# Gate rows of the second projection: split fp32r products against plain fp32 products in 32-column groups of TensorE

## The reference, cut to what matters

```python
# odd_mixer, layer 2 (w_in: 1024 x 5136, the last 16 columns are the gates)
q, k, v, o, z, g = split(h @ w_in)
g = (g + gate_bias).reshape(b, t, 4, MLSTM_HEADS)
gates = (g[:, :, 0], log_sigmoid(g[:, :, 1]), g[:, :, 2], log_sigmoid(g[:, :, 3]))
# mlstm_scan, per chunk of 128 rows
cum = cumsum(lf)
d_log = where(mask, cum_t - cum_s + li_s, -inf)
inter = cum + m
m_t = maximum(inter, max(d_log))
```

## Time and profile before

| | |
|---|---|
| median of three runs | 4188.26 us |
| lowest and highest | 4185.9 and 4190.44 us |
| profiled execution, its own time | 4191.84 us |
| span in the profile | 4190.2 us |
| PE matmul busy | 3694.5 us, 88% of the span |
| DVE, POOL, ACT busy | 2302.2, 1455.7, 1339.0 us |
| granted PE clock, mean | 0.929 |

### The profile page before, as it was taken

The page is one execution under the profiler, slowest core; times in us unless marked ns, Lnnn a source line. Parts: engine busy times, 40 slices in busy tenths (PEclk is TensorE's granted clock), DMA queues, the critical chain, the costliest instruction groups (busy, mean ns, idle before and its releaser), DMA issues. The chain is left out here.

```text
span 4190.2 us, 51199 instructions
## 1 busy us (share of the span) xinstructions
PE 3694.5 (88%) x17280; PEld 2784.6 (66%) x17280; DVE 2302.2 (55%) x3742; ACT 1339.0 (32%) x1955; POOL 1455.7 (35%) x964
## 2 busy tenths in 40 slices
PE   7999966589999999999189699999999968988687
PEld 4788754456666666665178588888877756876575
DVE  4533239756667676765637653333344335777555
ACT  3322225324444444444110132222223223655200
POOL 1100027336777767677203311000100002333243
PEclk8999986679999999999599899999999987999898
DMA  5212128511111111110244332221111115555443
GB/s 183 93 70 69 56 97 288 158 35 31 38 32 37 37 32 38 31 38 23 91 143 179 131 108 72 70 69 68 68 46 51 34 42 167 185 192 203 162 175 115
DMA packets 278209, 393.60 MB, mean 94 GB/s; under 512 B 79612, under 2 KB 167212, under 8 KB 277888
## 3 DMA queue, kind: packets, MB, share of 16 engines
q1 hardware_dynamic: 220256, 303.64, 22.1%
q10 hardware_dynamic: 47392, 50.50, 3.9%
q0 software_dynamic: 10368, 36.97, 2.2%
HBM read 269.71 MB, written 121.20 MB: 93 GB/s over the span
## 5 line engine op out<-in xcount | busy, mean ns | idle before, releaser
L235 PE MATMUL pj_acc<-pj_whi,pj_h_hi 128*128 128x512 f32 x2064 | 813.4, 394 | 22.8 <-DVE pj_h_lo L481 22.8
L237 PE MATMUL pj_acc<-pj_whi,pj_h_lo 128*128 128x512 f32 x2064 | 808.6, 392 | 0.0
L236 PE MATMUL pj_acc<-pj_wlo,pj_h_hi 128*128 128x512 f32 x2064 | 808.4, 392 | 0.0
L1017 DVE TENSOR_REDUCE al_mx<-al_sx 128x1 f32<-128x512 f32 (+1 forms) x960 | 562.3, 632 | 267.3 <-PE al_sx L1094 254.1
L962 ACT ACTIVATE al_e<-al_st 128x1024 f32<-128x1024 f32 x432 | 443.1, 1026 | 577.3 <-PE al_st L1107 567.8
L481 DVE TENSOR_TENSOR pj_h_lo<-pj_hall,pj_h_hi 128x1024 fp32r<-128x1024 f32 x258 | 369.2, 1432 | 352.2 <-ACT pj_h_hi L369 352.2
L431 POOL TENSOR_TENSOR pj_wlo<-pj_wst,pj_whi 128x2048 fp32r<-128x2048 f32 x28 | 128.5, 4588 | 975.8 <-ACT pj_whi L351 975.8
L992 POOL TENSOR_TENSOR al_acc_p<-al_acc_p,al_e 128x1024 f32<-128x1024 f32 x192 | 457.5, 2383 | 19.7
L235 PEld LDWEIGHTS pj_acc<-pj_whi,pj_h_hi 128*128 128x128 f32 x2064 | 391.2, 190 | 106.5 <-DVE pj_h_lo L481 26.2
L237 PEld LDWEIGHTS pj_acc<-pj_whi,pj_h_lo 128*128 128x128 f32 x2064 | 390.6, 189 | 82.4
L236 PEld LDWEIGHTS pj_acc<-pj_wlo,pj_h_hi 128*128 128x128 f32 x2064 | 391.1, 189 | 80.8
(11 more groups left out here) (256 smaller groups left out, 5554.8 us busy)
## 6 DMA issues: line engine op xcount, KB each, us to landing
s_proj<-pj_stage SPq DMA_DIRECT2D x194, 256.0 KB, 2.1
pj_wst<-in_w ACTq DMA_DIRECT2D x28, 1024.0 KB, 5.4
ml_k<-s_proj SPq DMA_DIRECT2D x36, 512.0 KB, 5.7
ml_v<-s_proj SPq DMA_DIRECT2D x36, 512.0 KB, 9.6
mo_in<-s_proj SPq DMA_DIRECT2D x34, 512.0 KB, 5.9
hm_w<-in_ada_w SPq DMA_DIRECT2D x16, 1024.0 KB, 6.6
ml_q<-s_proj SPq DMA_DIRECT2D x32, 512.0 KB, 7.7
s_h<-ml_h POOLq DMA_DIRECT2D x32, 512.0 KB, 5.7
```

The costliest lines, as they stand in the source:

```text
L235: nc.tensor.matmul(out, s_hi, m_hi, start=start, stop=False)
L236: nc.tensor.matmul(out, s_hi, m_lo, start=False, stop=False)
L237: return nc.tensor.matmul(out, s_lo, m_hi, start=False, stop=stop)
L1017: V.tensor_reduce(mx[:, x:x + 1], slots[x % NSX][:, 0:spans[x % NS][1]], AX.X, ALU.max).then_inc(sx_max, 1)
```

## The change

The gate weights become one tile `wg` of 32 columns for each of the eight slices of the inner dimension, not split. The gate product of a tile becomes eight plain fp32 matmuls on `hall` itself: slices 0 to 3 go to the PSUM partitions 0 to 31, 32 to 63, 64 to 95 and 96 to 127, and slices 4 to 7 are added to the same four. So `gacc` holds four partial sums of the 16 gate rows, in 128 rows; the bias goes to the first. `graw` keeps its size. The gate stage loads all four parts (16 transfers in place of four) and adds them, the forget gates on DVE and the input gates on POOL. PE's gate product now waits for `hall` of its tile; ACT's `h_hi` no longer waits for gate products.

```diff
         sg = m.sb(tag + "sg", [P, CH])
-        wg_hi, wg_lo = m.sb(tag + "wg_hi", [P, KD, P], F32R), m.sb(tag + "wg_lo", [P, KD, P], F32R)
+        wg = m.sb(tag + "wg", [P, KD, 32])
         gst, gbias = m.sb(tag + "gst", [P, 2, P]), m.sb(tag + "gbias", [P, 1])
         gacc = m.ps(tag + "gacc")
-        g_ld, g_hi, g_lo = m.sem(tag + "g_ld"), m.sem(tag + "g_hi"), m.sem(tag + "g_lo")
+        g_ld = m.sem(tag + "g_ld")
         g_mm, g_out, g_stored = m.sem(tag + "g_mm"), m.sem(tag + "g_out"), m.sem(tag + "g_stored", 2)
         sg_done, sgz_done = m.sem(tag + "sg_done"), m.sem(tag + "sgz_done")
-        wg_st = hall[:, KP:KP + 2, NT - 4:, :]
-        by_tile = lambda w: w[:].rearrange("p (a b) n -> p a b n", a=2)
     x_ld, stats_done, var_done, rstd_done, xn_done = m.sem(tag + "x_ld", NX), m.sem(tag + "stats_d"), m.sem(tag + "var"), m.sem(tag + "rstd_d"), m.sem(tag + "xn")
...
             eng.wait_ge(w1_hi, 1)
-            if not L0:
-                eng.wait_ge(g_lo, 1)
 
...
                     act.wait_ge(mm_done, k - RING + 1)
-                    if not L0 and k - RING < NT:
-                        act.wait_ge(g_mm, k - RING + 1)
                 nc.scalar.activation(h_hi[:, k % RING], hall[:, :, t, :], ACT.Copy).then_inc(hi_done, 1)
...
             if not L0:
-                for i in range(2):
-                    act.dma_start(wg_st[:, i], a["w_gate"][i * KP * P:(i + 1) * KP * P].rearrange("(k p) n -> p k n", p=P)).then_inc(g_ld, 16)
+                act.dma_start(wg[:], a["w_gate"].rearrange("(k p) n -> p k n", p=P)).then_inc(g_ld, 16)
                 act.dma_start(gbias[:], a["gate_bias"]).then_inc(g_ld, 16)
...
             split_w(1)
-            if not L0:
-                act.wait_ge(g_ld, 48)
-                nc.scalar.activation(by_tile(wg_hi), wg_st, ACT.Copy).then_inc(g_hi, 1)
             modulate(1)
...
                         act.wait_ge(g_mm, t + 1)
+                        act.wait_ge(g_ld, 32)
                         if t >= 2:
...
             low_w(0)
-            if not L0:
-                pool.wait_ge(g_ld, 48)
-                pool.wait_ge(g_hi, 1)
-                nc.gpsimd.tensor_tensor(by_tile(wg_lo), wg_st, by_tile(wg_hi).bitcast(F32), ALU.subtract).then_inc(g_lo, 1)
             for n in range(2, NT):
...
                     if t == 0:
-                        pe.wait_ge(g_lo, 1)
+                        pe.wait_ge(g_ld, 32)
                     else:
                         pe.wait_ge(g_out, t)
-                    for i in range(KD):
-                        mm = split_mm(nc, gacc[:, 0:P], wg_hi[:, i, :], wg_lo[:, i, :], h_hi[:, r, i, :], h_lo[:, r, i, :], i == 0, i == KD - 1)
+                    pe.wait_ge(hf_dve, t + 1)
+                    pe.wait_ge(hf_act, t + 1)
+                    for half in range(2):
+                        for g in range(4):
+                            i = 4 * half + g
+                            mm = nc.tensor.matmul(gacc[32 * g:32 * g + 32, 0:P], wg[:, i, :], hall[:, i, t, :], start=(half == 0), stop=(half == 1))
                     mm.then_inc(g_mm, 1)
...
     li, lf, tmp, cum, av, cmax, big, wgt, itr, low = (grid(n) for n in ("li", "lf", "tmp", "cum", "av", "cmax", "big", "wgt", "itr", "low"))
+    parts = [m.sb(f"gr_parts{d}", [HC, 2, 4, P]) for d in range(2)]
+    f_sum, i_sum = m.sem("gr_f_sum", 2), m.sem("gr_i_sum", 2)
     m_in_c, m_last_c = grid("m_in_c", 1), grid("m_last_c", 1)
...
             for d in range(2):
-                for dst, row in ((lf[d], 64 + 32 * d), (li[d], 32 * d)):
-                    sp.dma_start(dst[:], s["graw"][row:row + MH, :].rearrange("h (c n) -> (h c) n", n=P)).then_inc(ld, 16)
+                for kind, row in enumerate((8 + 4 * d, 4 * d)):
+                    for g in range(4):
+                        sp.dma_start(parts[d][:, kind, g, :], s["graw"][32 * g + row:32 * g + row + MH, :].rearrange("h (c n) -> (h c) n", n=P)).then_inc(ld, 16)
             sp.wait_ge(ready, 9)
...
                 nc.gpsimd.memset(t[:], 0.0).then_inc(ready, 1)
+            pool.wait_ge(ld, 256)
+            for d in range(2):
+                nc.gpsimd.tensor_tensor(parts[d][:, 1, 0:2, :], parts[d][:, 1, 0:2, :], parts[d][:, 1, 2:4, :], ALU.add).then_inc(i_sum[d], 1)
+                pool.wait_ge(i_sum[d], 1)
+                nc.gpsimd.tensor_tensor(li[d][:], parts[d][:, 1, 0, :], parts[d][:, 1, 1, :], ALU.add).then_inc(i_sum[d], 1)
 
...
         def _(act):
-            act.wait_ge(ld, 64)
             for d in range(2):
+                act.wait_ge(f_sum[d], 2)
                 nc.scalar.activation(tmp[d][:], lf[d][:], ACT.Abs).then_inc(soft[d], 1)
...
 
-            dve.wait_ge(ld, 64)
+            dve.wait_ge(ld, 256)
             for d in range(2):
+                V.tensor_tensor(parts[d][:, 0, 0:2, :], parts[d][:, 0, 0:2, :], parts[d][:, 0, 2:4, :], ALU.add).then_inc(f_sum[d], 1)
+                dve.wait_ge(f_sum[d], 1)
+                V.tensor_tensor(lf[d][:], parts[d][:, 0, 0, :], parts[d][:, 0, 1, :], ALU.add).then_inc(f_sum[d], 1)
+            for d in range(2):
+                dve.wait_ge(f_sum[d], 2)
                 step = 1 if d == 0 else -1
...
                 do(V.tensor_tensor_scan(cum[d][:, ::step], low[d][:, ::step], big[d][:, ::step], 0.0, ALU.mult, ALU.add))
+                dve.wait_ge(i_sum[d], 2)
                 do(V.tensor_tensor(av[d][:], li[d][:], cum[d][:], ALU.subtract))
...
     a["w1"] = np.concatenate([w[:, D:3 * D], w[:, 0:D], oz], 1)
-    wg = np.zeros((D, P), w.dtype)
+    wg = np.zeros((D, 32), w.dtype)
     gb = np.zeros((P, 1), odd_gate_bias.dtype)
-    for kind, row in ((0, 0), (1, 64), (2, 32), (3, 96)):
+    for kind, row in ((0, 0), (1, 8), (2, 4), (3, 12)):
         wg[:, row:row + MH] = w[:, 5 * D + kind * MH:5 * D + (kind + 1) * MH]
```

## The result

The changed kernel takes 4162.81 us, the median of four runs (4158.31 to 4166.11), where the kernel before took 4189.35 beside it (four runs, 4185.9 to 4193.05). The ratio is 0.9936, with a 95% interval from 0.9919 to 0.9953: 26.5 us faster. The forecast was 4165.0, 23.3 us less.

A forecast was written before the change was run, and what follows sets the result against it. PE was taken to bound the second projection's first column block, while added gate-stage steps are paid in full. -35.6 + 6.6 - 0.7 + 6.4 = -23.3 us from the median 4188.26 gave 4165.0 us, range 4157 to 4183.

The forecast's parts named there:

- The gate products: Second projection's first column block: eight plain fp32 matmuls take 0.65 us a tile, not 2.63; 18 tiles save 35.6 us.
- The two changes of width: PE's switches between full-width and 32-column work around each tile's gate products: an estimated 0.1 us each.
- emptying: Rival: a matmul must end wholly before another width begins, 0.34 us a tile; total 4167; chance 0.14.
- Part 2: First column block: PE's room before transposes shrinks from 2.79 to 0.81 us, so disturbances give back 6.6 us.
- (a): PE's wait where ACT's weight split and POOL's delay DVE's `h_lo`: delay of 5.27 us will cost 4.46, 2.0 more.
- (b): ACT's weight split in turn 12, 1.9 us, with no PE wait before: 1.1 us given back.
- (c): POOL's second weight split, beside DVE's normalising: PE's wait grows from 1.08 to 3.07 us, 2.0 more.
- The clock: Given back: one more half-clock spell, 1.5 us. As rival: whole turns at 1.2 GHz, each 7.0 us more; chance 0.07.
- The start: Before PE's first main matmul: gate-weight splits on ACT and POOL are gone, so DVE's low part ends sooner; saves 0.7 us.
- The gate stage: Twelve more transfers cost 4.8 us and the additions 1.6: 6.4 us lost, 4.8 to 12 at the bounds.
- Each record its 0.11 us: Rival: column groups gain nothing at this width, gate products take 1.78 us a tile; total 4180.4; chance 0.18.
- The chain becomes the bound: Rival: `h_hi` starts no earlier, so a turn takes 7.6 us, 11.8 us lost together; total 4176.8; chance 0.09.

The follow-up runs named there:

- again: The changed kernel once more, unedited: 4164.16 us, ratio 0.9938.
- one_group: The changed kernel with a tile's eight gate products all on the first 32 partitions, and the old gate stage: 4182.24 us, ratio 0.998.
- full_width: The changed kernel with gate weights padded to 128 columns, eight full-width plain fp32 products, and the old gate stage: 4171.65 us, one run.
- pool_late: The changed kernel with POOL's additions in the gate stage made to wait until DVE has done its own: 4166.97 us, one run.
- four_loads: The changed kernel with the gate stage's sixteen transfers merged into four: 4156.04 us, one run.
- split_later: The changed kernel with ACT's weight splits moved behind the next turn's `h_hi` and modulation: 4134.44 us, one run.

## Why the prediction was right

The sum was -23.3 us and the medians give -26.5. In the two parts of the span that the change touches it was -24.2 in the first profile and -22.8 in again, so the sum fits there, and the rest is scatter of parts that the change leaves alone. Term by term:

- **The gate products, 18 x 1.98 = 35.6.** Right: 18 x 1.95 = 35.1. A turn is 7.06 us where 7.03 was forecast; block and entry are 0.58 + 0.09 = 0.67, where I had 0.65. Taking the lower end, because the earlier trace rows show records of different groups starting together, was the right choice: one_group shows what the upper end would have been, 1.86 us, and only without the groups.
- **The two changes of width, 0.1 us each.** 0.25 together by full_width against one_group. Slightly under-sized, and the direction of the *emptying* rival was right, but not its 0.34.
- **Part 2, 6.6 us given back.** By the lengths of the three turns it is 4.9 us in the first profile and 6.5 in again (5.4 in pool_late and in four_loads). So it was over-sized by 0.1 to 1.7 us. The waits were: 4.45, 0.82 and 2.15 against 2.48, 0 and 1.08 before are 2.0 + 0.8 + 1.1 = 3.9, where I had 5.1. (a) was right and (b) 0.3 too long. At (c) I used the ordinary room of 0.81 us, but (b) stands one turn ahead of (c), and (c)'s chain runs on while PE waits there, so (c) has 0.82 us more; split_later shows it, where (b) is gone and (c) is 3.02 us. The clock, 1.5, cost 1.1 us more than before in the first profile, 1.6 in pool_late, 1.5 in four_loads and 2.6 in again, where PE ran at half clock for 6.8 us from (a) on and for another 3.4 behind (c). That again comes within 0.1 of 6.6 is luck, as its two misses cancel. Only the first profile lacks the second spell, and why it does stays open.
- **The start, 0.7.** First load to first main matmul went from 24.40 to 23.85 us, 0.55 less; DVE's low part took 2.25 us without POOL beside it, where it took 3.00. Another 0.4 lie between the first main matmul and the first gate product. Together 1.0.
- **The stretch together.** -35.6 + 6.6 - 0.7 = -29.7 was forecast. Measured, -35.1 + 4.9 - 1.0 = -31.2 in the first profile and -35.1 + 6.5 - 1.0 = -29.6 in again.
- **The gate stage, 6.4.** 7.0, and 6.8 in again. Twelve issues cost 5.3 in place of 4.8, and the additions 1.7 in place of 1.6; 0.54 of that is DVE beside POOL by pool_late, which I had bounded at 2 and put at nothing, so the additions by themselves were over-sized. The 2.5 us for POOL's four does not follow from its 4.6 us for 2048 columns, which gives 1.7 for their 768; they ran for 3.0, beside DVE's.
- **Rivals.** *Each record its 0.11 us* is false in four groups and true in one. *The chain becomes the bound* is false: `h_hi` moved ahead with the gate products, and an ordinary turn shows no wait. *The clock* is false as it was put, with whole turns at half clock and the gain gone: the granted clock of the stretch is 0.97 in the first profile and 0.96 in again, and the spells stand behind PE's waits, not at the gate products.

## What to carry to other kernels

Products with few output columns are worth packing side by side when the engine is bound by its streams: here four groups made eight products three times as fast, for 0.25 us of changes of width per visit and one addition stage later, in which every extra transfer issue was paid in full. Count both sides first: 15 of the 24 us came from the plain fp32 products alone, and the groups added 8 to 9. And before a change that shrinks PE's turn, list what the other engines do in long single instructions: the room that covers them shrinks too, and here cutting one POOL instruction into four brought more (43 us) than the change itself (26.5).

## What the runs showed of the hardware

- A 2048-column subtraction on POOL (4.60 us) held a DVE subtraction of 1024 columns for its whole length (4.86 in place of 1.23); in pieces of 512 columns DVE took 1.54, and POOL 5.99. I had priced this in the first column block and missed the 22.8 us of PE's idle time that it causes in the later ones. Behind three of those waits PE fell to half clock, which with the waits made 25 us in the second projection.
- The same code with the same wait of 2.1 us at (c) was followed by a half-clock spell in three profiles (1.6 us each) and by none in one.
- A gate block's weight loads cost nothing to be seen: 128 columns of weights for each product took no longer than 32 (1.78 against 1.86 us).
- With four merged transfers DVE started 5.4 us after the first issue, on one queue or on two, with the 16 DMA engines 0.81 to 0.87 busy at the peak; with sixteen single ones, issued over 6.5 us, it started 1.8 us after the last.
